# Neighbourhood attention in tiles of 16 grid rows by 8 grid columns, with every token layout following those tiles

## The chip, the cores and the metric

The kernel runs on one core of one Trainium2 chip. The time is the device time of one execution in microseconds (us): three runs of the kernel before gave a median of 2781.56 us, from 2779.58 to 2782.93 us. The profiled execution took 2779.84 us; its span, from the first to the last instruction, is 2778.1 us, so 1.7 us lie around the span.

## The reference, cut to what matters

One encoder layer is applied to 1024 prompt tokens (a grid of 16 rows by 64 columns) and, apart from them, to 256 sample tokens (4 rows by 64 columns). All arithmetic is float32, and the kernel gets it from pairs of rounded numbers (a high and a low part).

```
h = rms_norm(x);  qA,kA,vA,qB,kB,vB = split(h @ w_in)             # 1024 -> 6 x 512
# A: neighbourhood attention, 8 heads of 64; per token 8 grid rows x 16 grid columns of keys
row_start = clip(r - 4, 0, rows - 8);  col_start = clip(c - 8, 0, 64 - 16)
s = q.k / 8 + rpb[h, key_row - r + 7, key_col - c + 15];  outside the window: -inf
yA = rms_norm(softmax(s) @ v)
# B: differential attention, 4 heads, all tokens of the sequence are keys
s = q.k / 8 + t5_table[bucket(k_pos - q_pos)]                     # depends on the distance alone
yB = rms_norm((softmax(s1) - lam * softmax(s2)) @ v)
x = x + concat(yA, yB) @ w_out
x = x + expert_choice(rms_norm(x))      # 16 experts, each takes its 2n/16 best tokens
y = rms_norm(x)
```

`top_k` in the router keeps the lower token number where two affinities are equal, so the kernel has to count chosen tokens in the order of their numbers.

## The kernel before, in words

Tokens are handled in `TT` = 10 tiles of 128: prompt tiles 0 to 7 (128 consecutive tokens, that is two grid rows) and sample tiles 8 and 9. The program goes through these stages: load and normalise the ten tiles of `x` and turn them (`x_tile`, `x_tile_turn`); the values of half the heads (`v_tile`); the projection of keys and queries for the first job (`project(0, c, ...)`); then 80 attention steps, the output projection with router, the choice of tokens, and 16 experts, which take the last 1.9 ms.

A step `s` is one tile `t = s % 10` of one job `j = s // 10`. Jobs 0 to 3 are neighbourhood attention (`s < NAS`, two heads a job), jobs 4 to 7 differential attention. The order on TensorE in a neighbourhood step is written out: `scores(s)`, `values(s - 2)`, half of `project_part` (a share of the next job's key and query projection), `turn_exps(s - 1, ...)` (transposes of the exponentials in groups of at most 4 blocks, each into one of two buffers `PT`), the other half of `project_part`, and `out_turn(s - 2)`. VectorE adds the bias table and takes the maximum (`bias_max`), ScalarE takes the exponentials (`exps`), copies the turned blocks (`turned_copy`) and rounds weights (`w_round`). ScalarE and VectorE also go through the steps in a fixed order: in steps with `t` in (6, 7) of job `j`, ScalarE rounds the two halves of the unit of weights `(j + 2, 1)`, after the exponentials and copies of that step, and everything behind it on ScalarE waits for it.

How many keys a step has is set by `na_window(t)`. Two grid rows of queries see at most nine grid rows of keys, 576, for tiles 2 to 5; tiles 0, 1, 6 and 7 see 512; sample tiles see 256. Keys are taken by blocks of 128, the last block of a 576-key step being half full.

The bias of neighbourhood attention is laid out in memory as `G_d` (`bias_rows`), written once from GpSimd (L1920), and read back per job by `na_table(j)` on the SyncE queue as four loads into `TE` (L529). GpSimd adds the column mask and copies the nine rows of inner tiles to `TI` (`bias_tables`). The table of differential attention is a row of 2048 numbers a head, `F_d` (`t5_rows`), written from GpSimd as four rows of 2048 numbers (L1925), spread to `Fs_d` (`t5_shifted`), from which `df_table(h)` reads 128 rows of 1920 numbers in one load (L532).

The SyncE queue issues its transfers one after another in the order of the code. `unit(...)` loads one 512 KB piece of `w_in` into the single buffer `w_st` (L495), after the piece before it has been split (`w_split`); `w_round` waits for the load by the count of `w_in`.

After the output projection the chosen tokens are counted on TensorE (L883, `count`): one matmul with a triangular matrix inside tiles, and matmuls with a matrix of ones for the tiles before.

Of the kernel before, what the change touches and what calls it, by code (L numbers as in the profile page):

```python
# [8 lines left out]
F32 = mybir.dt.float32  # L9
# [6 lines left out]
P = 128  # L16
# [6 lines left out]
GW = 64  # L23
# [22 lines left out]

def na_window(t):

    if t >= TPR:
        return TPR, NSA, 7 - 2 * (t - TPR), False  # L50
    if t < 2:
        return 0, 512, 7 - 2 * t, False
    if t < 6:
        return t - 2, 576, 3, True
    return 4, 512, 3 - 2 * (t - 6), False


def na_blocks(t):
    return -(-na_window(t)[1] // P)
# [121 lines left out]
def build(nc, x_prompt, x_sample, mix_norm_w, w_in, na_rpb, na_norm_w, t5_table, lambda_q1,  # L181
# [10 lines left out]
    Fs_d = nc.dram_tensor("t5_shifted", (DF_H, P, 2 * NPR + P), F32).ap()  # L192
# [7 lines left out]
    def x_rows(t):  # L200
        return xp[t * P:(t + 1) * P, :] if t < TPR else xs[(t - TPR) * P:(t - TPR + 1) * P, :]
# [43 lines left out]
    TE = [at(f"TE{b}", [P, 2, 16, GW], F32, (150 + 8 * b) * K) for b in range(2)]  # L245
    TI = at("TI", [P, 2, 9 * GW], F32, 166 * K)
    BT = [at("BT0", [P, 1920], F32, 166 * K), at("BT1", [P, 1920], F32, 150 * K)]
    E0 = 173 * K + 512
    En = at("En", [P, 4, 640], F32, E0)
# [13 lines left out]
    t5_p = at("t5_p", [DF_H, 2 * NPR], F32, 80 * K)  # L263
    msk_w = at("msk_w", [P, 8, GW], F32, E0 + 29 * K)
# [4 lines left out]
    mask = after("mask", [P, GW], F32)  # L269
    ssx = after("ssx", [P, 2 * TT], F32)  # L270
# [40 lines left out]
    one = at("one", [P, P], BF16, 77 * K + 896)  # L311
    g_rest = at("g_rest", [P, TT, NE], F32, 79 * K)
# [68 lines left out]
    G_out, F_out, Fs_out = sem("G_out"), sem("F_out"), sem("Fs_out")  # L381
# [20 lines left out]
    te_in, bt_in = [sem("te_in0"), sem("te_in1")], [sem("bt_in0"), sem("bt_in1")]  # L402
    table_ready, te_clear = sem("table_ready"), sem("te_clear")
# [76 lines left out]
    with nc.Block() as block:  # L480
# [3 lines left out]
        def _(sp):  # L484
# [13 lines left out]
            def x_tile(t):  # L498
                if t >= 4:
                    sp.wait_ge(turned, 2 * (t - 3))  # L500
                sp.dma_start(xin[t % 4], x_rows(t)).then_inc(x_in[t % 4], 16)
# [36 lines left out]
            unit((1, 0), (2, 1), (2, 0))  # L538
# [6 lines left out]
            sp.wait_ge(scores_read, 2 * (3 * TT + 6))  # L545
            sp.wait_ge(Fs_out, 16)
# [3 lines left out]
            df_table(1)  # L550
            unit((5, 0), (6, 1), (6, 0))
            sp.wait_ge(scores_read, 2 * (NAS + TT))
            df_table(2)
            unit((7, 1), (7, 0))
            sp.wait_ge(scores_read, 2 * (NAS + 2 * TT))
            df_table(3)

# [7 lines left out]
            def mixed_rows(t):  # L565
# [3 lines left out]
                sp.dma_start(xt[:, t % 2, :], x_rows(t)).then_inc(y_in[t % 2], 16)  # L569
# [48 lines left out]
        def _(pe):  # L618
# [56 lines left out]
            def scores(s):  # L675
# [7 lines left out]
                if s < NAS:  # L683
                    kt0, nk, _, inner = na_window(t)
# [14 lines left out]
            def exp_blocks(s):  # L699
# [6 lines left out]
                return [En[:, 2 * (s % 2) + hf, b * P:min(nk, (b + 1) * P)] for hf in range(2) for b in range(na_blocks(t))]  # L706
# [13 lines left out]
            def values(s):  # L720
# [6 lines left out]
                if s < NAS:  # L727
                    kt0, nk, _, _ = na_window(t)
                    nb = na_blocks(t)
                    for b in range(nb):  # L730
                        n = min(P, nk - b * P)
                        for hf in range(2):
                            mm = pe.matmul(O[64 * hf:64 * hf + 64, 0:P],
                                           V[0:n, kt0 + b, cols.start + 64 * hf:cols.start + 64 * hf + 64],
                                           PTs[0:n, hf * nb + b, :], start=(b == 0), stop=(b == nb - 1))
# [33 lines left out]
            for s in range(NAS):  # L769
# [7 lines left out]
                if s >= 1:  # L777
                    turn_exps(s - 1, (2,))
# [107 lines left out]
            for t0, t1 in ((0, TPR), (TPR, TT)):  # L886
                for t in range(t0, t1):
                    if t + 1 < t1:
                        count(ranks[:, :, t + 1:t1, :], one,
                              chosen[:, :, t, :].unsqueeze(2).to_broadcast([P, 2, t1 - t - 1, NE]))  # L890
                    mm = count(ranks[:, 1, t0:t1, :], one,
                               chosen[:, 0, t, :].unsqueeze(1).to_broadcast([P, t1 - t0, NE]), last=t == TT - 1)
# [480 lines left out]
        def _(dve):  # L1373
# [49 lines left out]
            def window_mask():  # L1423
                dve.wait_ge(const_ready, 1)
                A, C = msk_w[:, 0, :], msk_w[:, 1, :]
# [80 lines left out]
            def na_bias(s):  # L1506

                j, t = s // TT, s % TT
                _, nk, row, inner = na_window(t)
# [8 lines left out]
                for hf in range(2):  # L1518
                    e = En[:, 2 * (s % 2) + hf, :]
                    if inner:  # L1520
                        bias_max(s, hf, S[:, hf, :].rearrange("p (b n) -> p b n", b=2)[:, :, 0:288],
                                 TI[:, hf, :].rearrange("p (b n) -> p b n", b=2),
                                 e[:, 0:576].rearrange("p (b n) -> p b n", b=2))
                    else:
# [657 lines left out]
```

## Time and profile before

| engine | busy, us | share of the span |
|---|---|---|
| TensorE (PE) | 2678.6 | 96% |
| TensorE weight loads (PEld) | 2521.4 | 91% |
| VectorE (DVE) | 1978.8 | 71% |
| ScalarE (ACT) | 1715.2 | 62% |
| GpSimd (POOL) | 1096.0 | 39% |

Profiled execution 2779.84 us, span 2778.1 us, mean granted TensorE clock 0.986 of full speed. The forty neighbourhood steps run from 112.4 us to about 348 us of the span; a job (ten steps) takes 59.2 us once it is steady. The differential steps begin at 409.8 us, the experts at about 862 us.

How to read it: "busy" is time in which an instruction was under way; a matmul's end is modelled and its length overlaps the next one, so what a group of matmuls costs is read from the start of the group to the start of the next. SyncE's own row does not count as busy; what it issues is seen as transfers.

### The profile page before, as it was taken

How to read it: one execution, taken by the hardware profiler on the slowest of the kernel's cores; microseconds unless marked ns; L12 is line 12 of the kernel's file. 1: busy time of each engine (PE TensorE's matmuls, PEld its weight loads, DVE VectorE, ACT ScalarE, POOL GpSimd, SP SyncE). 2: the span in 40 equal slices, each digit the busy share in tenths (PEclk: the TensorE clock that was granted, in tenths of full speed). 3: DMA queues.
4: the chain of work that ended last, by engine and by line, in shares of the span. 5: the costliest groups of instructions: out<-in, count | busy, mean ns of one | idle time of the engine just before them, and what ended most of it. 6: DMA issues, size and time to landing. Idle time of an engine off the chain costs nothing. (4 is left out here: it accounts for less than half of the span.)

```text
span 2778.1 us, 54432 instructions
## 1 busy us (share of the span) xinstructions
PE 2678.6 (96%) x22988; PEld 2521.4 (91%) x22988; DVE 1978.8 (71%) x2350; ACT 1715.2 (62%) x2559; POOL 1096.0 (39%) x738
## 2 busy tenths in 40 slices
PE   7999999998986999999999999999999999999996
PEld 7877898877876999999999999999999999999996
DVE  5233326666467878878788787887878788787787
ACT  3366615555124676767667676676767767676675
POOL 2132220224112453636446263452735436364352
PEclk9999999999987999999999999999999999999998
DMA  7231110113354889889888898879888888898887
GB/s 190 52 101 40 48 55 30 40 56 104 139 225 163 311 277 332 285 316 318 289 308 285 318 315 309 314 260 335 300 308 313 286 321 285 318 315 289 321 284 282
DMA packets 357644, 655.40 MB, mean 236 GB/s; under 512 B 25752, under 2 KB 85016, under 8 KB 356888
## 3 DMA queue, kind: packets, MB, share of 16 engines
q1 hardware_dynamic: 341291, 606.41, 61.2%
q0 software_dynamic: 16112, 45.53, 6.1%
q8 instruction: 183, 3.00, 0.4%
q14 instruction: 58, 0.47, 0.0%
HBM read 616.48 MB, written 39.62 MB: 236 GB/s over the span
## 5 line engine op out<-in xcount | busy, mean ns | idle before, releaser
L1776 DVE TENSOR_TENSOR wl<-stg,wh 128x2048 bf16<-128x2048 f32 (+1 forms) x544 | 1243.9, 2292 | 276.5 <-ACT wh L1298 271.9
L1298 ACT ACTIVATE wh<-stg 128x2048 fp32r<-128x2048 f32 (+1 forms) x544 | 1010.9, 1861 | 203.4 <-PE S L944 78.9
L2120 POOL TENSOR_TENSOR hx<-hh,hx 128x320 fp32r<-128x320 f32 x176 | 384.8, 2186 | 814.7 <-ACT hx L1350 814.4
L941 PE MATMUL S<-X,wh 128*128 128x320 f32 x3760 | 591.9, 312 | 1.3 <-DVE X L1785 1.3
L941 PEld LDWEIGHTS S<-X,wh 128*128 128x128 f32 x3760 | 556.3, 188 | 3.9 <-issue 2.1
L987 PE MATMUL S<-hx,wh 128*128 128x320 f32 x1892 | 312.4, 313 | 4.9 <-DVE yTs L1824 4.9
L941 PE MATMUL OG<-X,wh 128*128 128x320 f32 x1872 | 298.4, 312 | 0.0
L944 PE MATMUL S<-Xb,wl 128*128 128x160 bf16 x3760 | 290.1, 233 | 0.0
L987 PEld LDWEIGHTS S<-hx,wh 128*128 128x128 f32 x1892 | 280.8, 188 | 6.8 <-issue 6.7
L941 PEld LDWEIGHTS OG<-X,wh 128*128 128x128 f32 x1872 | 277.2, 188 | 1.3 <-issue 1.1
L944 PEld LDWEIGHTS S<-Xb,wl 128*128 128x128 bf16 x3760 | 258.9, 98 | 12.0
L2122 POOL CAST hb<-hx 128x320 bf16<-128x320 f32 x176 | 202.9, 1153 | 0.0
L1350 ACT ACTIVATE hx<-hh 128x320 fp32r<-128x320 f32 x176 | 83.1, 472 | 176.0 <-DVE hh L1813 176.0
L1968 POOL TENSOR_TENSOR ca<-lsum,half 128x20 f32<-128x20 f32 (+3 forms) x10 | 24.2, 2420 | 393.6 <-ACT o_all L1191 241.0
L987 PE MATMUL OG<-hx,wh 128*128 128x320 f32 x924 | 158.0, 313 | 1.9 <-DVE yTs L1824 1.9
L944 PE MATMUL S<-hb,wl 128*128 128x160 bf16 x1892 | 158.8, 233 | 0.0
L1159 ACT ACTIVATE E<-E,nmax 128x1024 f32<-128x1024 f32 (+1 forms) x80 | 81.8, 1023 | 110.0 <-DVE nmax L1503 110.0
L944 PE MATMUL OG<-Xb,wl 128*128 128x160 bf16 x1872 | 149.2, 233 | 0.0
L630 PE MATMUL OG<-hT_h,wkq 128*128 128x512 f32 (+1 forms) x384 | 149.1, 388 | 0.1
L987 PEld LDWEIGHTS OG<-hx,wh 128*128 128x128 f32 x924 | 138.6, 188 | 2.6 <-issue 2.6
L944 PEld LDWEIGHTS S<-hb,wl 128*128 128x128 bf16 x1892 | 132.1, 98 | 8.1
L632 PE MATMUL OG<-hT_h,wkq 128*128 128x512 f32 (+1 forms) x384 | 136.9, 356 | 0.0
(283 smaller groups left out, 4262.4 us busy)
## 6 DMA issues: line engine op xcount, KB each, us to landing
stg<-in_w_gate_dram SPq DMA_DIRECT2D x80, 2048.0 KB
stg<-in_w_up_dram SPq DMA_DIRECT2D x80, 2048.0 KB
stg<-in_w_down_dram SPq DMA_DIRECT2D x64, 2048.0 KB
stg<-in_w_down_dram SPq DMA_DIRECT2D x32, 1536.0 KB
stg<-in_w_gate_dram SPq DMA_DIRECT2D x16, 1024.0 KB
stg<-in_w_up_dram SPq DMA_DIRECT2D x16, 1024.0 KB
w_st<-in_w_in_dram SPq DMA_DIRECT2D x20, 512.0 KB, 3.8
yt<-mixed SPq DMA_DIRECT2D x10, 512.0 KB, 4.5
```

What stands on the lines that cost most here:

```text
L630: pe.matmul(out, lhs_h, rhs_h, start=first, stop=False)
L632: return pe.matmul(out, lhs_l, rhs_h, start=False, stop=last)
L941: pe.matmul(out, w, x, start=first, stop=False, skip_group_check=True)
L944: return pe.matmul(out[:, 0:CT], w, x, start=False, stop=last, skip_group_check=True)
L987: mm = pe.matmul(down_bank(e, d), whk[:, f, c * P:(c + 1) * P], hx[:, f0 + f, :], start=(f0 + f == 0), stop=(last and f0 + f == FT - 1), s ...
L1159: act.activation(e, e, ACT.Exp, scale=-1.0, bias=nmax[:, col:col + 1], accum_out=lsum[:, j % 2, t, hf:hf + 1]).then_inc(exp_done, 1)
L1298: act.activation(piece_conv(wh, g), piece_stage(g), ACT.Copy).then_inc(rounded, 1)
L1350: act.activation(hx[:, j - 1:j + 1, 0:CT], hh[:, :, :], ACT.Copy).then_inc(hidden_hi, 1)
L1776: dve.tensor_tensor(piece_conv(wl, g), piece_stage(g), piece_conv(wh, g).bitcast(F32), ALU.subtract).then_inc(split, 1)
L1968: own(pool.tensor_tensor(a, ls, minus_one, ALU.pow))
L2120: pool.tensor_tensor(hx[:, f, CT:2 * CT], hh[:, :, :], hx[:, f, 0:CT].bitcast(F32), ALU.subtract).then_inc(hidden_ready, 1)
L2122: pool.tensor_copy(hb[:, f, :], hx[:, f, 0:CT].bitcast(F32)).then_inc(hidden_b, 1)
```

## The change

Prompt tiles 0 to 7 become blocks of 16 grid rows by 8 grid columns (an octet of columns each). A tile's queries then see the keys of its own octet and its neighbours: 384 keys, or 256 for the first and last tile. The tokens of a tile come by a rearranged load of `x`, and results of the output projection are stored back by the rearranged pattern. The bias tables become: `TB`, five variants of 128 by 128 a head, put together from `TR`, which is loaded by 16 small loads a head; `TS` for the sample tiles; for differential attention `W_d` (`t5_octets`), written from `F_d` by 32 transfers of 31 x 15 runs of 8 numbers, from which `df_table` now loads its table in 16 pieces; and `BS` for the sample tiles. The counting of chosen tokens goes by grid rows inside and across tiles.

```diff
 def na_window(t):
     if t >= TPR:
-        return TPR, NSA, 7 - 2 * (t - TPR), False
-    if t < 2:
-        return 0, 512, 7 - 2 * t, False
-    if t < 6:
-        return t - 2, 576, 3, True
-    return 4, 512, 3 - 2 * (t - 6), False
+        return TPR, NSA
+    first, last = max(t - 1, 0), min(t + 1, TPR - 1)
+    return first, (last - first + 1) * P
+def row_start(r):
+    return min(max(r - NA_KH // 2, 0), GR - NA_KH)      # GR = 16, OC = 8
...
+    W_d = nc.dram_tensor("t5_octets", (DF_H, OC, 2 * TPR - 1, 2 * GR - 1, OC), F32).ap()
+    Fs_d = nc.dram_tensor("t5_shifted", (DF_H, P, NSA + 3 * P), F32).ap()
-    Fs_d = nc.dram_tensor("t5_shifted", (DF_H, P, 2 * NPR + P), F32).ap()
+    def octet(prompt, sample, t):
+        if t < TPR:
+            return prompt.rearrange("(r g c) d -> g r c d", r=GR, c=OC)[t]
+        return sample[(t - TPR) * P:(t - TPR + 1) * P, :]
...
             def na_table(j):
                 for hh_ in range(2):
+                    q = (2 * j + hh_) * NDR
                     for up in range(2):
-                        q = (2 * j + hh_) * NDR
-                        src = G_d[:, q:q + NDR, GW - 1:2 * GW - 1]
-                        sp.dma_start(TE[j % 2][GW * up:GW * up + GW, hh_, up:up + NDR, :], src).then_inc(te_in[j % 2], 16)
+                        sp.dma_start(TS[j % 2][GW * up:GW * up + GW, hh_, :, :],
+                                     G_d[:, q + 5 - up:q + 11 - up, GW - 1:2 * GW - 1]).then_inc(te_in[j % 2], 16)
+                    for r in range(GR):
+                        r0 = row_start(r)
+                        d0 = q + r0 - r + NA_KH - 1
+                        sp.dma_start(TR[j % 2][OC * r:OC * r + OC, hh_, r0:r0 + NA_KH, :],
+                                     G_d[0:OC, d0:d0 + NA_KH, GW - 1 - OC:GW - 1 + 2 * OC]).then_inc(te_in[j % 2], 16)
+            def t5_octets(h):
+                for c in range(OC):
+                    src = bass.AP(F_d.tensor, F_d.offset + h * 2 * NPR + OC - 1 - c,
+                                  [[GW, 2 * GR - 1], [OC, 2 * TPR - 1], [1, OC]])
+                    sp.dma_start(W_d[h, c].rearrange("g r k -> r g k"), src).then_inc(W_out, 16)
             def df_table(h):
-                sp.dma_start(BT[h % 2][:, :], Fs_d[h, :, P - 1:P - 1 + 1920]).then_inc(bt_in[h % 2], 16)
+                for r in range(GR):
+                    sp.dma_start(BT[h % 2][OC * r:OC * r + OC, :].rearrange("c (g q) -> c g q", q=P),
+                                 W_d[h, :, :, GR - 1 - r:2 * GR - 1 - r, :].rearrange("c g r k -> c g (r k)")
+                                 ).then_inc(bt_in[h % 2], 16)
...
             na_table(0)
             na_table(1)
-            unit((1, 0), (2, 1), (2, 0))
+            unit((1, 0))
+            sp.wait_ge(F_out, 16)
+            for h in range(DF_H):
+                t5_octets(h)
+            unit((2, 1), (2, 0))
...
-                    k0, chunks = kt0 * P, [(0, 0, 288), (512, 288, 288)] if inner else [(0, 0, nk)]
+                    k0, chunks = kt0 * P, [(0, 0, nk)]
...
                 project_part(s, 1)
-                if s >= 1:
-                    turn_exps(s - 1, (2,))
...
-            for t0, t1 in ((0, TPR), (TPR, TT)):
-                for t in range(t0, t1):
-                    if t + 1 < t1:
-                        count(ranks[:, :, t + 1:t1, :], one, ...)
-                    mm = count(ranks[:, 1, t0:t1, :], one, ..., last=t == TT - 1)
+            for t in range(TPR):
+                if t + 1 < TPR:
+                    n = TPR - t - 1
+                    count(ranks[:, 0, t + 1:TPR, :], one, chosen[:, 0, t, :].unsqueeze(1).to_broadcast([P, n, NE]))
+                    count(ranks[:, 1, t + 1:TPR, :], row_le, chosen[:, 1, t, :].unsqueeze(1).to_broadcast([P, n, NE]))
+                if t:
+                    count(ranks[:, 1, 0:t, :], row_lt, chosen[:, 1, t, :].unsqueeze(1).to_broadcast([P, t, NE]))
+                count(ranks[:, 1, 0:TPR, :], one, chosen[:, 0, t, :].unsqueeze(1).to_broadcast([P, TPR, NE]))
+            # the two sample tiles are counted as before: three matmuls
...
             def bias_tables(j):
-                pool.wait_ge(te_in[j % 2], 64 * (j // 2 + 1))
+                pool.wait_ge(te_in[j % 2], 16 * 2 * (2 + GR) * (j // 2 + 1))
...
+                own(pool.tensor_tensor(te, te, mask[:, :].unsqueeze(1).to_broadcast([P, 12, GW]), ALU.add))
+                for b, u, side in ((0, 0, None), (1, 0, 0), (2, 1, None), (3, 2, 1), (4, 2, None)):
+                    # one copy or one masked addition of 128 x 256 into TB
```

SyncE, from the weight loads ahead of the first bias tables on, before (a row names the line, the destination and source tensors, the shape of the destination and the count; `w_st` is the weight buffer, `TE` the bias table of a job):

```order
L495 DMA w_st<-in_w_in_dram 128x8x128 [waits w_split] x2
L529 DMA TE_71<-bias_rows 64x15x64 [waits te_clear,G_out]
L529 DMA TE_71<-bias_rows 64x15x64 x3
L529 DMA TE_72<-bias_rows 64x15x64 x4
L495 DMA w_st<-in_w_in_dram 128x8x128 [waits w_split] x3
```

The same place with the change, where `TS` and `TR` are parts of a job's tables and `t_octets` is `W_d`:

```order
L518 DMA w_st<-in_w_in_dram 128x8x128 [waits w_split] x2
L551 DMA TS_73<-bias_rows 64x6x64 [waits te_clear,G_out]
L551 DMA TS_73<-bias_rows 64x6x64
L556 DMA TR_75<-bias_rows 8x8x24 x16
L551 DMA TS_73<-bias_rows 64x6x64 x2
L556 DMA TR_75<-bias_rows 8x8x24 x16
L551 DMA TS_74<-bias_rows 64x6x64 x2
L556 DMA TR_76<-bias_rows 8x8x24 x16
L551 DMA TS_74<-bias_rows 64x6x64 x2
L518 DMA w_st<-in_w_in_dram 128x8x128 [waits w_split]
L564 DMA t_octets<-t_rows 31x15x8 x31
L518 DMA w_st<-in_w_in_dram 128x8x128 [waits w_split] x2
```

Eight loads ahead of unit (1, 0) have become 72, and between unit (1, 0) and unit (2, 1) stand 32 transfers from memory to memory that were not there (the first of them, and the last group of `TR`, are left out of the fence).

TensorE, scores and values of step 5 of job 0, before (`K_h` and `K_l` are the key parts, `PTs` the turned exponentials):

```order
L695 MATMUL S<-K_h,Qh 128x288 [waits fill_split,scores_read]
L695 MATMUL S<-K_h,Qh 128x288
L695 MATMUL S<-K_l,Qh 128x288 x2
L695 MATMUL S<-K_h,Ql 128x288 x2
L695 MATMUL S<-K_h,Qh 128x288 x2
L695 MATMUL S<-K_l,Qh 128x288 x2
L695 MATMUL S<-K_h,Ql 128x288 x2
L733 MATMUL OG<-PTs,V 64x128 [waits out_read,turned_copied]
L733 MATMUL OG<-PTs,V 64x128 x9
```

The same step with the change:

```order
L745 MATMUL S<-K_h,Qh 128x384 [waits fill_split,scores_read]
L745 MATMUL S<-K_h,Qh 128x384
L745 MATMUL S<-K_l,Qh 128x384 x2
L745 MATMUL S<-K_h,Ql 128x384 x2
L781 MATMUL OG<-PTs,V 64x128 [waits out_read,turned_copied]
L781 MATMUL OG<-PTs,V 64x128 x5
```

Twelve score matmuls of 288 columns are now six of 384, and ten value matmuls are six; the waits at the head of each group are the same.

## Rows read from the trace of the kernel before

**Rows 1.** Busy time by stretch: PE, PEld, DVE, ACT, POOL, clock, DMA share, GB/s.

```profile
170.00:229.00 59.00, 59.00 (x479) 47.45 (x478) 18.41 (x50) 38.39 (x132) 20.65 (x14) 1.00 0.20 46
...
840.00:2778.00 1938.00, 1892.11 (x17402) 1854.36 (x17402) 1575.67 (x1470) 1332.85 (x1518) 905.27 (x523) 0.99 0.85 300
```

**Rows 2.** Timeline of PE, first scores and job 1: start, length, what.

```profile
112.40 0.50 PE L695 MATMUL S<-K_h,Qh 64*128 64x512 f32 x2
...
169.94 0.50 PE L695 MATMUL S<-K_h,Qh 64*128 64x512 f32 x2
...
170.84 0.66 PE L733 MATMUL OG<-PTs,V 128*64 128x128 f32 x8
171.43 0.50 PE L630 MATMUL OG<-hT_h,wkq 128*128 128x512 f32 x1
...
180.38 0.40 PE L695 MATMUL S<-K_h,Qh 64*128 64x288 f32 x2
...
181.37 1.09 PE L733 MATMUL OG<-PTs,V 128*64 128x128 f32 x16
182.39 0.50 PE L630 MATMUL OG<-hT_h,wkq 128*128 128x512 f32 x1
...
200.19 1.46 PE L733 MATMUL OG<-PTs,V 128*64 128x128 f32 x20
201.58 0.50 PE L630 MATMUL OG<-hT_h,wkq 128*128 128x512 f32 x1
...
205.32 0.38 PE L625 MATMUL PT<-identf,En 128*128 128x128 f32 x2
205.54 0.27 PE L625 MATMUL PT<-identf,oTs 128*128 128x128 f32 x1
...
218.44 0.39 PE L695 MATMUL S<-K_h,Qh 64*128 64x256 f32 x2
...
218.99 1.09 PE L733 MATMUL OG<-PTs,V 128*64 128x128 f32 x16
...
229.18 0.50 PE L695 MATMUL S<-K_h,Qh 64*128 64x512 f32 x2
```

**Rows 3.** Timeline of the SyncE queue, issues from the constants to the first tables.

```profile
35.15 0.43 SPq L518 DMA_DIRECT2D lam_v<-in_lambda_q_dram  x1
...
78.46 9.18 SPq L529 DMA_DIRECT2D TE<-bias_rows  x8
106.75 54.89 SPq L495 DMA_DIRECT2D w_st<-in_w_in_dram  x3
```

**Rows 4.** The line of the table loads: ns of one issue, min/median/max.

```profile
L529 SPq DMA_DIRECT2D TE<-bias_rows x16: 585/774/1576, 78.5 to 228.1; - x16
```

**Rows 5.** The line that rounds weights on ScalarE, in job 0.

```profile
L1099 ACT ACTIVATE wkq<-w_st x4: 622/638/659, 121.7 to 159.9; 128x512 fp32r<-128x512 f32 x4
```

**Rows 6.** Timeline of ScalarE, end of step 6 of job 0.

```profile
154.28 0.66 ACT L1099 ACTIVATE wkq<-w_st 128x512 fp32r<-128x512 f32 x1
```

**Rows 7.** Timeline of GpSimd: the mask added to the first bias table.

```profile
86.98 4.60 POOL L1939 TENSOR_TENSOR TE<-TE,mask 128x2048 f32<-128x2048 f32 x1 [27.10 <-DMA TE<-bias_rows]
```

**Rows 8.** Transfers by size (columns as Rows 1): w_st; TE; w_st with BT.

```profile
186.00:195.00 9.00, 9.00 (x87) 7.07 (x85) 3.58 (x9) 5.81 (x22) 8.55 (x5) 1.00 0.21 60
165.50:174.50 9.00, 9.00 (x74) 7.58 (x72) 2.99 (x10) 5.51 (x22) 0.00 (x0) 1.00 0.63 109
338.00:346.00 8.00, 8.00 (x71) 6.69 (x66) 2.75 (x10) 4.99 (x19) 0.00 (x0) 1.00 0.53 190
```

**Rows 9.** The page's issues: KB each, median us from issue to landing.

```profile
w_st<-in_w_in_dram SPq DMA_DIRECT2D x20, 512.0 KB, 3.8
...
bias_rows<-rpb_p POOLq DMA_DIRECT2D x1, 3840.0 KB, 29.1
...
t_rows<-t_p POOLq DMA_DIRECT2D x1, 32.0 KB, 14.0
```

**Rows 10.** Timeline of PE, the counting of chosen tokens.

```profile
844.49 1.89 PE L883 MATMUL S<-chosen,one 128*128 128x224 bf16 x18
```

More of the change, by code:

```diff
@@ L705, in exp_blocks @@
                 nk = na_window(t)[1]
-                return [En[:, 2 * (s % 2) + hf, b * P:min(nk, (b + 1) * P)] for hf in range(2) for b in range(na_blocks(t))]
+                return [En[:, 2 * (s % 2) + hf, b * P:(b + 1) * P] for hf in range(2) for b in range(nk // P)]
             def turn_exps(s, fills):
@@ L885, in _ @@
             count(S[:, 1, 0:2 * TT * NE], tri, chosen[:, :, :, :].rearrange("p m t e -> p (m t e)"), first=True)
-            for t0, t1 in ((0, TPR), (TPR, TT)):
-                for t in range(t0, t1):
-                    if t + 1 < t1:
[L889 to L892, printed above, removed]
+            for t in range(TPR):
[6 more added lines that the diff above has]
+                count(ranks[:, 1, 0:TPR, :], one, chosen[:, 0, t, :].unsqueeze(1).to_broadcast([P, TPR, NE]))
+            for t in range(TPR, TT):
+                if t + 1 < TT:
+                    count(ranks[:, :, t + 1:TT, :], one,
+                          chosen[:, :, t, :].unsqueeze(2).to_broadcast([P, 2, TT - t - 1, NE]))
+                mm = count(ranks[:, 1, TPR:TT, :], one,
+                           chosen[:, 0, t, :].unsqueeze(1).to_broadcast([P, TT - TPR, NE]), last=t == TT - 1)
             mm.then_inc(pos_ps, 1)
@@ L1508, in na_bias @@
                 j, t = s // TT, s % TT
-                _, nk, row, inner = na_window(t)
+                nk = na_window(t)[1]
                 if t == 0:
@@ L1901, in _ @@
             own.wait()
+            own(pool.iota(msk_c[:, :], [[0, GR], [1, OC]], base=0, channel_multiplier=0,
+                          allow_small_or_imprecise_dtypes=True))
+            own.wait()
             pool.sem_inc(const_ready, 1)
@@ L1934, in bias_tables @@
             def bias_tables(j):
-                pool.wait_ge(te_in[j % 2], 64 * (j // 2 + 1))
+                pool.wait_ge(te_in[j % 2], 16 * 2 * (2 + GR) * (j // 2 + 1))
                 pool.wait_ge(mask_ready, 1)
-                te = TE[j % 2][:, :, :, :].rearrange("p h r c -> p (h r) c")
-                own(pool.tensor_tensor(te, te, mask[:, :].unsqueeze(1).to_broadcast([P, 32, GW]), ALU.add))
-                own.wait()
-                if j:
-                    pool.wait_ge(scores_read, 2 * ((j - 1) * TT + 6))
-                stand()
-                for h in range(2):
-                    own(pool.tensor_copy(TI[:, h, :], TE[j % 2][:, h, 3:12, :].rearrange("p r c -> p (r c)")))
-                own.wait()
-                stand()
-                own(pool.memset(TI[0:GW, :, 8 * GW:9 * GW], MASKED))
-                own(pool.memset(TI[GW:P, :, 0:GW], MASKED))
+                stand()
+                te = TS[j % 2][:, :, :, :].rearrange("p h r c -> p (h r) c")
+                tr = TR[j % 2][:, :, :, :].rearrange("p h r u -> p (h r) u")
+                own(pool.tensor_tensor(te, te, mask[:, :].unsqueeze(1).to_broadcast([P, 12, GW]), ALU.add))
+                for b, u, side in ((0, 0, None), (1, 0, 0), (2, 1, None), (3, 2, 1), (4, 2, None)):
+                    out = TB[j % 2][:, b, :, :].rearrange("p h (r c) -> p (h r) c", c=OC)
+                    cols = tr[:, :, OC * u:OC * u + OC]
+                    if side is None:
+                        own(pool.tensor_copy(out, cols))
+                    else:
+                        own(pool.tensor_tensor(out, cols,
+                                               mask_lr[:, side, :].unsqueeze(1).to_broadcast([P, 2 * GR, OC]), ALU.add))
                 own.wait()
@@ L2013, in list_constants @@
                 own(pool.memset(one[:, :], 1.0))
+                own(pool.memset(row_le[:, :], 1.0))
+                own(pool.memset(row_lt[:, :], 1.0))
                 own(pool.memset(posm[:, :, NE:NE + 2], 0.0))
@@ L2032, in list_constants @@
                 own(pool.memset(NG[:, :, NE:NE + 2, 2:PARTS], 0.0))
+                own.wait()
+                for rows, base in ((row_le, OC), (row_lt, 0)):
+                    own(pool.affine_select(out=rows[:, :], in_=rows[:, :], compare_op=ALU.is_gt, fill=0.0, base=base,
+                                           pattern=[[OC, GR], [0, OC]], channel_multiplier=-1))
                 own.wait()
```

105 lines of the change are left out of this document (71 added, 34 removed).

## The prediction

> **What bounds the kernel now.** Read the busy times by stretch first. In the second job of neighbourhood attention TensorE is busy for 59.00 of 59.00 us, while VectorE has 18.41, ScalarE 38.39 and GpSimd 20.65; the experts, 1938 us of the span, have TensorE busy for 1892 us [rows 1]. So in the stretch that the change touches, the other engines hide behind TensorE, and a matmul that goes is time that goes, as long as no wait takes its place. The experts are the same code on the same shapes; I take their time as unchanged. The second view is TensorE's timeline, read from the start of one group to the start of the next [rows 2]. The third is SyncE: it issues in order, so what stands ahead of a weight load delays it [rows 3]. The fourth is where those weight loads are waited for on ScalarE [rows 5, 6].
>
> **What TensorE saves.** Per neighbourhood step, from [rows 2]:
> - Scores to the next group: 0.90 us with 512 keys (169.94 to 170.84), 0.99 with 576 (180.38 to 181.37), 0.55 with 256 (218.44 to 218.99). For 384 I take the middle of 256 and 512, 0.725.
> - Values: 0.59 us for two blocks (170.84 to 171.43; the trace counts two passes a matmul, so x8 is two blocks for two heads), 1.02 for four (181.37 to 182.39), 1.39 for five with the half one (200.19 to 201.58). Three blocks: 0.805.
> - Transposes: 0.22 for two (205.32 to 205.54), 0.11 each; four, two or four of them go.
>
> A job has two tiles that go from 512 keys to 256, two from 512 to 384, four from 576 to 384, and two sample tiles that stay. Scores: 2 x 0.35 + 2 x 0.175 + 4 x 0.265 = 2.11. Values: 2 x 0.43 + 2 x 0.215 + 4 x 0.585 = 3.63. Transposes (eight to four, eight to six, ten to six): 2 x 0.44 + 2 x 0.22 + 4 x 0.44 = 3.08. That is 8.8 us a job and 35.3 us for four jobs. Could another engine take over? ScalarE's 38.4 us a job is below the 59.2 - 8.8 = 50.4 that a job would last (59.2 from 169.94 to 229.18 [rows 2]), and its exponentials and copies shrink too; VectorE and GpSimd are further off [rows 1]. No loss there.
>
> **What is added.** Counting: the 18 matmuls with ones took 1.89 us, 0.105 each [rows 10]. There are now 3 + 6 x 4 + 2 = 29 for the prompt and 3 for the sample, 14 more, and VectorE waits for the last: +1.5 us. The first load of x is now a pattern of 16 x 8 rows; an issue may cost the 0.77 us of a table load instead of 0.43 [rows 3, 4]: +0.3 us at the start. GpSimd's extra constants stand ahead of the third output tile, and rearranged stores keep rows of 4 KB: nothing, covered by output-projection matmuls, at most 1 or 2 us.
>
> So without a new wait: 2779.8 - 35.3 + 1.5 + 0.3 = 2746.3 us. The profiled execution lies 1.7 us under the median of the runs, within their spread, so I make no correction.
>
> **SyncE's queue.** The eight table loads were issued from 78.46 on [rows 3]. Now 8 TS loads at 0.77 us (6.2 us) [rows 4] and 64 TR loads at 0.47 us from issue to issue (0.43 and a gap, the nearest small load) [rows 3], 30.1 us: the last at 114.8. The first job's half is out at 96.6. With 5 us to land and GpSimd's work (4.60 us for 2048 columns makes 1.7 for the 768 of TS, and about 0.5 for each of five pieces of 256 columns) [rows 7], the table stands at about 106, ahead of the first scores at 112.4 [rows 2]. Unit (1, 0) goes out at 115 instead of 106.75 and lands 3.8 us later [rows 3, 9], at 119, just ahead of its first use at 121.7 [rows 5]. Both hidden, with 2 to 6 us to spare.
>
> Then come the 32 transfers of `t5_octets`, 31 x 15 = 465 runs of 32 bytes each: 14,880 packets. Unit (2, 1) stands behind all of them, and ScalarE wants it at the end of step 6. That was at 154.28 [rows 6]; by then TensorE has saved about 6 us, so at 148. All that ScalarE does behind this rounding waits with it: the exponentials of step 7 and the copy that frees `out_turn`. TensorE stops within one step.
>
> What does a packet cost? By DMA share times 16 engines times the stretch [rows 8]: 0.21 x 144 = 30.2 us for the 1024 packets of 512 bytes of `w_st`, 29.5 ns each; 0.63 x 144 = 90.7 us for the 3840 packets of 256 bytes of `TE`, 23.6 ns; 0.53 x 128 = 67.8 us, less 30.2 for a `w_st`, for the 128 rows of 7680 bytes of `BT`, 294 ns. The line through 256 and 512 bytes gives 18.4 ns at 32 bytes; the line through 512 and 7680 gives 11.8. Upper bound: the 7680 runs of 512 bytes that `bias_rows` wrote to memory took 29.1 us with all overhead [rows 9], 480 an engine, 61 ns. I take 18.4, from the sizes nearest to 32 bytes.
>
> How many engines share them? No row shows a transfer whose outer dimension is 31. Dealt evenly over 16 engines the packets last 14,880 x 18.4 / 16 = 17 us, and the 32 issues (25 us at 0.77) are what one sees. All on one engine they last 274 us. The row nearest to the question is `t_rows`: four rows, 32 KB, 14.0 us to landing, where 512 KB in 128 rows take 3.8 us [rows 9]. Its queue also held the tail of `bias_rows`, so it proves little, but it does say that a transfer with a small or odd outer dimension can't be taken to spread as one of 128 rows does. 31 splits into equal parts only by 1 and 31, while the quick transfers have 64 or 128 rows, which 16 divides. I take one engine.
>
> The Trainium skill, "DMA: Bandwidth & Descriptors", section "Why a DMA increments its semaphore by 16 and not by 1", says that a transfer uses the largest number up to 16 that divides the outer dimensions of both sides. By that rule 31 gives one engine, always the lowest, and this term is the 274 us; if the rule did not hold here it would be the 17 us. No row shows either.
>
> The single engine's ring also holds its part of every later SyncE load, so unit (2, 1) can't land before it is drained: 115 + 274 + 4 = 393 us. Wanted at 148: a stall of 245 us, once. After it, `W_d` is complete, the later units and tables are a job ahead of their use, and differential attention finds its tables. The `BT` tables in 16 pieces of 120 runs of 512 bytes: 1920 x 29.5 ns, even on eight engines 7 us, and they have a job's time. Sum: 2746.3 + 245 = 2991 us.
>
> With 11.8 ns the packets last 176 us, the stall is 147 and the time 2893; with 61 ns they last 908, and the time is 3625. The same page's specification table asks for at least 512 bytes a transfer and says that below this the engine reads, modifies and writes. By that rule the 32-byte writes would cost more than the loads I extrapolate from; no row here shows a small store to memory by itself.
>
> **The rivals.**
> - The packets are spread over 16 engines (or nearly so). 25 us of issue from 115 on, unit (2, 1) lands at 144, four us ahead of 148: 2746 us, faster by 1.2%. For it: every transfer whose landing the page gives is quick for its size but `t_rows`. Against: 31.
> - The packets are spread, but the many issues cost more than I take, 0.77 us each as for table loads. The 72 last 55 us, the first table is ready at about 115 instead of 112.4 (+3), unit (1, 0) lands at 138 instead of 121 (+17, the larger one counts for both): about 2763, faster by 0.6%.
> - The saving isn't had: a short step is bound by the chain from scores over VectorE and ScalarE to the transposes. It speaks against it that TensorE never waited in the rows of job 1. Then 2780, no change, if the octets don't matter either.
> - On the other side of these stands the forecast itself, one mechanism: unit (2, 1) behind `t5_octets`, decisive from the point at which the drain lasts longer than 148 - 119 = 29 us, or 1.9 ns a packet on one ring, and slower overall from 66 us, 4.5 ns a packet.
>
> **How the numbers follow.** Chances: one engine, slower, 0.79 (its own range 2880 to 3300, from 11 to 39 ns a packet); spread and quick, 0.13; spread with late issues, 0.05; no saving, 0.03. The predicted time is that of the first, 2991 us. The range goes down to 2742 to take in the spread cases and up to 3300; what is left out is the single engine above 39 ns. Faster or slower is meant beyond 0.2%, 5.6 us, which is about what the measurement tells from no change: faster 0.18, same 0.03, slower 0.79.
>
> **What would show it.** Right: PE idle in one block near 145 us with ScalarE's `w_st` rounding waiting for a DMA; SyncE's issue of `t_octets` drawn out; DMA share near one sixteenth (0.06) through that stretch; neighbourhood jobs 2 to 4 at 50 to 51 us each. Wrong: `t_octets` landing within some 30 us of its issue; jobs that still last over 55 us; a new wait in the output projection or at the first scores. A stall of the right place with another length means that the price of a packet was off, nothing else.

## The result and the profile after

The changed kernel takes 2909.55 us (median of 4 runs, 2905.96 to 2910.76), the kernel before 2780.90 us in the 4 runs beside them (2779.58 to 2782.93). The ratio is 1.046, 95% interval 1.0442 to 1.0478: slower, as forecast, by 129 us where 211 were forecast. 2909.55 lies in the range of the one-engine case (2880 to 3300), near its lower end.

SyncE's queue after, at the place of [rows 3] (start, length, line and what; times in us):

```profile
81.17 1.30 SPq L551 DMA_DIRECT2D TS<-bias_rows  x2
82.52 5.74 SPq L556 DMA_DIRECT2D TR<-bias_rows  x16
...
104.34 5.73 SPq L556 DMA_DIRECT2D TR<-bias_rows  x16
110.12 0.40 SPq L518 DMA_DIRECT2D w_st<-in_w_in_dram  x1
110.56 175.60 SPq L564 DMA_DIRECT2D t_octets<-t_rows  x32
286.21 15.54 SPq L518 DMA_DIRECT2D w_st<-in_w_in_dram  x2
...
526.59 11.08 SPq L568 DMA_DIRECT2D BT<-t_octets  x16
537.71 0.98 SPq L573 DMA_DIRECT2D BS<-t_shifted  x2
538.74 51.75 SPq L518 DMA_DIRECT2D w_st<-in_w_in_dram  x3
```

The 32 octet copies hold SyncE for 175.60 us: 5.49 us each, 11.8 ns for each of the 14,880 packets. Unit (2, 1) goes out at 286.21. The last two copies had not landed by then: the last landings that the trace records for their semaphore `W_out` stand at 289.2 and 294.4 us. ScalarE could start on unit (2, 1) at 295.33, 9.1 us after its issue, where 3.8 is usual [rows 9]. What the queue's standstill does stands in the waits from 100 to 450 us (engine, tile and line that waited, what ended the wait; us in total, times, longest):

```profile
ACT wkq L1152 <- DMA w_st<-in_w_in_dram: 144.5, 1, 144.5
PE PT L675 <- ACT PTs L1223: 144.1, 1, 144.1
```

One wait of ScalarE for the weights, and one of TensorE of the same length. ScalarE's row answers to [rows 6]; TensorE's timeline has the end of the stall, and then the starts of two jobs, to be read against the 59.24 us of a job in [rows 2]:

```profile
295.33 0.63 ACT L1152 ACTIVATE wkq<-w_st 128x512 fp32r<-128x512 f32 x1 [144.49 <-DMA w_st<-in_w_in_dram]
```

```profile
298.94 0.45 PE L675 MATMUL PT<-identf,oTs 128*128 128x128 f32 x1 [144.13 <-ACT PTs L1223]
...
312.03 0.39 PE L745 MATMUL S<-K_h,Qh 64*128 64x256 f32 x2
...
363.01 0.39 PE L745 MATMUL S<-K_h,Qh 64*128 64x256 f32 x2
```

A job now lasts 50.98 us, 8.26 less than before. By stretch (columns as in [rows 1]):

```profile
150.00:296.00 146.00, 4.77 (x36) 3.51 (x32) 0.70 (x2) 1.47 (x7) 0.00 (x0) 0.53 0.13 6
296.00:303.00 7.00, 4.06 (x22) 3.12 (x23) 2.74 (x10) 4.46 (x18) 0.00 (x0) 0.50 0.06 14
303.00:309.00 6.00, 5.75 (x34) 4.41 (x34) 1.37 (x5) 2.10 (x8) 0.00 (x0) 0.79 0.25 74
```

In the stall the granted clock fell to the lower level, 0.5 or 1.2 GHz, and it was still there when TensorE had work again at 298.94. A mean of 0.79 from 303 to 309 puts its rise at about 305.5. These 6.6 us at half the clock cost some 3 us.

The whole difference of the two spans, 130.9 us, divides so (each part is the difference of a distance between two starts):

| stretch | before | after | difference |
|---|---|---|---|
| to the first scores | 112.40 | 115.11 | +2.7 |
| first scores to first differential scores | 297.43 | 412.06 | +114.6 |
| from there to the first output tile | 271.67 | 279.40 | +7.7 |
| output tiles, first to last | 135.98 | 140.45 | +4.5 |
| last output tile to the end | 1960.62 | 1961.98 | +1.4 |

The second line is 144.1 us of stall and some 3 us of low clock, less 33 us that the steps save. The third shows in the waits from 520 to 560 us: behind the 16 `BT` loads of 526.59 to 537.7 above, unit (5, 0) comes late, and TensorE waits 6.3 us in turn.

```profile
ACT wkq L1152 <- DMA w_st<-in_w_in_dram: 7.9, 1, 7.9
...
PE S L745 <- DVE nmax L1564: 6.3, 1, 6.3
```

The fourth is the load of `x` for the residual, by its line, after:

```profile
L619 SPq DMA_DIRECT2D xt<-in_x_prompt_dram x8: 547/548/624, 765.5 to 888.2; - x8
L619 SPq DMA_DIRECT2D xt<-in_x_sample_dram x2: 332/332/333, 904.2 to 919.5; - x2
```

An issue of 16 groups of 8 rows takes 548 ns, one of 128 rows in a run 332 (before it was 327 or 328 for both). `yt` is issued behind it, and TensorE waits for the pair of them (`y_in` counts both) 7.1 us on 5 tiles, where it had been 1.5 us on 3.

### The profile page after: what moved, and what is told of

Same layout as the page of the kernel before. It is cut to its first block and busy times, and to the rows that moved or that the text cites. A ratio compares the mean times of both kernels' runs of the same rounds, so it can differ in the third digit from the quotient of the medians.

```text
span 2909.0 us, 53806 instructions
## 1 busy us (share of the span) xinstructions
PE 2650.7 (91%) x22570; PEld 2496.3 (86%) x22570; DVE 1971.1 (68%) x2355; ACT 1691.5 (58%) x2535; POOL 1089.4 (37%) x750
## 5 line engine op out<-in xcount | busy, mean ns | idle before, releaser
L1458 DVE TENSOR_TENSOR wkq<-w_st,wkq 128x512 fp32r<-128x512 f32 x36 | 29.8, 839 | 182.5 <-ACT wkq L1152 182.5
L680 PE MATMUL OG<-hT_h,wkq 128*128 128x512 f32 (+1 forms) x384 | 149.4, 389 | 2.1 <-DVE Ql L1546 1.5
L675 PE MATMUL PT<-identf,oTs 128*128 128x128 f32 x40 | 11.2, 280 | 145.1 <-ACT PTs L1223 144.1
## 6 DMA issues: line engine op xcount, KB each, us to landing
stg<-in_w_down_dram SPq DMA_DIRECT2D x32, 1536.0 KB, 11.1
```

What stands on the lines that cost most here:

```text
L680: pe.matmul(out, lhs_h, rhs_h, start=first, stop=False)
L1458: dve.tensor_tensor(lo[:, k, :], w_st[:, k, :], hi[:, k, :].bitcast(F32), ALU.subtract).then_inc(w_split, 1)
```

## The experiments

**The outer dimension of the copies.** The same packets to the same places, with 15 outside instead of 31.

```diff
-                                  [[GW, 2 * GR - 1], [OC, 2 * TPR - 1], [1, OC]])
-                    sp.dma_start(W_d[h, c].rearrange("g r k -> r g k"), src).then_inc(W_out, 16)
+                                  [[OC, 2 * TPR - 1], [GW, 2 * GR - 1], [1, OC]])
+                    sp.dma_start(W_d[h, c], src).then_inc(W_out, 16)
```

> The changed kernel with one edit: the 32 copies of the octet tables are described with the 15 groups as their outer dimension and the 31 row distances inside, the same 465 packets of 32 bytes each, to the same places. Theory one (each copy goes wholly to one DMA engine because 31 divides by nothing up to 16 but 1): now 15 engines share a copy, the 175.6 us that SyncE stood in these issues becomes about 12 us of transfer beside some 13 us of issues, unit (2,1) lands before 140 and ScalarE no longer waits 144.1 us for it; 2909.5 less 144.1 and less about 3 us of half clock behind the stall is 2762, with 2756 to 2770 as the range. Theory two (a copy from device memory to device memory in 32-byte packets costs 11.8 ns a packet in the queue itself, however many engines share it): the issues still take about 5.5 us each, the wait stays 144 us and the time 2905 to 2913.

Measured: 2759.61 us (2757.62 to 2764.82, 4 runs); ratio to before 0.9921, interval 0.9905 to 0.9938. SyncE's queue:

```profile
109.79 33.16 SPq L564 DMA_DIRECT2D t_octets<-t_rows  x32
142.99 13.47 SPq L518 DMA_DIRECT2D w_st<-in_w_in_dram  x2
```

The 144 us are gone, and with them 150 us of time, so the number of packets was not what cost. The issues take 33 us, not the 13 that I expected; unit (2, 1) at 142.99 is in time for ScalarE, which rounds it at 149.90 without a wait. The steps from the first scores to the first differential scores last 264.73 us against 297.43: without the stall the change saves 32.7 us there.

**The same copies cut by rows.** Here the order of the packets stays and only the count of rows in a copy changes. 31 is cut into 16 and 15, then into 17 and 14, 20 and 11, 25 and 6. The count that the queue later waits for on `W_out` is doubled with the copies (not shown).

```diff
-                    sp.dma_start(W_d[h, c].rearrange("g r k -> r g k"), src).then_inc(W_out, 16)
+                    dst = W_d[h, c].rearrange("g r k -> r g k")
+                    sp.dma_start(dst[:GR], src[:GR]).then_inc(W_out, 16)      # GR = 16; then 17, 20, 25
+                    sp.dma_start(dst[GR:], src[GR:]).then_inc(W_out, 16)
```

> The changed kernel, in which each octet copy of 31 rows is issued as two, of 16 rows and of 15 rows, 64 issues instead of 32; source, destination, order of the packets and their number stay. Theory one (the count 31 alone puts a copy on one engine): 16 and 15 engines share them; 64 issues of 0.36 to 0.5 us are 23 to 32 us from 110.6, unit (2,1) is issued by 134 to 143 and lands by 140 to 150 where ScalarE wants it at 151 (295.3 less the 144.5 of waiting), so the wait is 0 to 3 us and the time 2762 to 2768. Theory two (the order in which the packets read and write memory, row distance first, makes them slow): 64 issues of 2.7 us, the wait stays about 144 us, 2905 to 2915.

> As the copies cut into 16 and 15 rows, but cut into 17 and 14: 17 is prime. Theory one (the largest divisor up to 16 of the row count is the number of engines): the 17 rows, 255 packets, go to one engine, at 11.8 ns 3.0 us, and the pair takes 3.0 to 3.8 us, 32 of them 97 to 122 us from 110. Unit (2,1) then lands at 211 to 236, ScalarE wants it at 150.5, the wait is 60 to 86 us where 16 and 15 rows left 16.5, and the time 2779.8 plus 44 to 69: 2823 to 2849. A rival in which 31 is slow for its size or its packets and not for its divisors: 17 rows cost about what 16 do, 2776 to 2790.

> As above with 20 and 11 rows. Theory one (divisors): 10 engines and 11 engines, 30 and 15 packets each, a pair at 1.5 to 2.0 us, 48 to 64 us in all, a wait of 16 to 33 us, 2779 to 2797. The rival that more than 16 rows that 16 does not divide go to one engine: 300 packets at 11.8 ns are 3.5 us, a pair 3.6 to 4.3 us, a wait of 79 to 103 us, 2842 to 2866.

> As above with 25 and 6 rows. Theory one (divisors): 5 engines for the 25 rows, 75 packets each, at 11.8 ns 0.9 us, and 6 for the others; a pair at 1.5 to 2.2 us, 48 to 70 us, a wait of 16 to 39 us, 2779 to 2803. The rival that more than 16 rows go to one engine: 375 packets are 4.4 us, a wait of 106 to 133 us, 2869 to 2896.

Measured, one run each (the wait is ScalarE's for unit (2, 1)):

| rows | largest divisors up to 16 | time | wait | landings recorded |
|---|---|---|---|---|
| 31 (the change) | 1 | 2909.55 | 144.5 | 64 for 32 copies |
| 17 and 14 | 1 and 14 | 2835.59 | 73.0 | 544 for 64 |
| 25 and 6 | 5 and 6 | 2783.50 | 18.8 | 416 for 64 |
| 20 and 11 | 10 and 11 | 2782.55 | 19.9 | 736 for 64 |
| 16 and 15 | 16 and 15 | 2779.82 | 16.5 | 1024 for 64 |
| 15 outside | 15 | 2759.61 | none | 512 for 32 |

17 rows cost 52 to 53 us more than 25 or 20 rows do, so it is neither the size nor that 16 is passed. What sets 17 apart is that nothing up to 16 but 1 divides it. The queue shows it for 17 and 14 rows (L565 issues the 17, L566 the 14 behind them), and ScalarE's row its price:

```profile
126.27 0.60 SPq L565 DMA_DIRECT2D t_octets<-t_rows  x1
126.93 2.44 SPq L566 DMA_DIRECT2D t_octets<-t_rows  x1
```

```profile
222.63 0.63 ACT L1154 ACTIVATE wkq<-w_st 128x512 fp32r<-128x512 f32 x1 [72.95 <-DMA w_st<-in_w_in_dram]
```

It is the next issue that is held up, while the 255 packets on one engine drain: 0.60 and 2.44 and the gaps make 3.1 us, and over all 32 pairs 3.4, where 255 times 11.8 ns is 3.0. With 20 and 11 rows no issue is held up in the steady run, and a pair takes 1.57 us:

```profile
126.68 0.74 SPq L565 DMA_DIRECT2D t_octets<-t_rows  x1
127.46 0.75 SPq L566 DMA_DIRECT2D t_octets<-t_rows  x1
128.25 0.74 SPq L565 DMA_DIRECT2D t_octets<-t_rows  x1
```

My expectation of 0 to 3 us of wait for 16 and 15 rows was wrong: I priced an issue at 0.36 to 0.5 us, from the table loads, and these took 0.57 and 0.81 us in most pairs (and 0.04 from one to the next), some 47 us for 64. A few took up to 2.4 us, and all of them 53 us, from 109.96 to 162.82.

The landings that the trace records for the semaphore `W_out` fit one rule for all six: with k the largest divisor up to 16, a copy leaves k + 1 records where k is under 16, and 16 where it is 16. 32 x 2 = 64; 32 x (2 + 15) = 544; 32 x (6 + 7) = 416; 32 x (11 + 12) = 736; 32 x (16 + 16) = 1024; 32 x 16 = 512. All six counts come out. The Trainium skill, "DMA: Bandwidth & Descriptors", section "Why a DMA increments its semaphore by 16 and not by 1", says that each engine in use posts one and the issuing sequencer writes the remaining 16 - k in one step; by that rule the counts are these, and the trace agrees.

**Half of the copies.** The tables of heads 2 and 3 are read from those of heads 0 and 1, so that 16 copies do.

```diff
-            for h in range(DF_H):
+            for h in range(DF_H // 2):
                 t5_octets(h)
...                                    # df_table(h) reads W_d[h % 2]
```

> The changed kernel with 16 of the 32 octet copies: only those of the first two heads are made, and the tables of heads 2 and 3 are loaded from those of heads 0 and 1 (their bias is that of another head). Theory one (a queue of work on one engine that the weights behind it wait out, 5.49 us a copy): the wait shrinks by 16 times 5.49, 87.8 us, from 144.1 to about 56, and the time to 2909.5 less 87.8, 2822, range 2815 to 2828. A rival in which the wait is a fixed one for the last copy's completion, or is ended by something else, gives 2895 to 2910.

Measured: 2818.04 us. The queue and the wait:

```profile
110.35 87.67 SPq L564 DMA_DIRECT2D t_octets<-t_rows  x16
198.06 15.58 SPq L518 DMA_DIRECT2D w_st<-in_w_in_dram  x2
```

```profile
ACT wkq L1152 <- DMA w_st<-in_w_in_dram: 56.6, 1, 56.6
```

5.48 us a copy again, and the wait shrinks by 87.9 us with 87.9 us less in the queue. That leaves 3.6 us of the 91.5 gained. The stretch from the differential scores to the first output tile is 276.38 us here and not 279.40, and ScalarE's wait for unit (5, 0) in it 5.4 us and not 7.9, which holds 3.0 of them; why that wait was shorter isn't shown.

**The kernel before with the copies added.** No tile is changed; nothing reads the result.

```diff
-            unit((1, 0), (2, 1), (2, 0))
+            unit((1, 0))
+            sp.wait_ge(F_out, 16)
+            for h in range(DF_H):
+                for c in range(8):
+                    src = bass.AP(F_d.tensor, F_d.offset + h * 2 * NPR + 7 - c, [[GW, 31], [8, 15], [1, 8]])
+                    sp.dma_start(W_d[h, c].rearrange("g r k -> r g k"), src).then_inc(W_out, 16)
+            unit((2, 1), (2, 0))
```

> The kernel before the change with one addition: the 32 octet copies of the change, in its form with 31 rows outside, behind unit (1,0) on SyncE's queue; nothing reads what they write, and the queue waits for them ahead of the first dilated table. Theory one (the copies alone make the loss, whatever the tiles are): SyncE stands about 175 us from about 109, less the slack before ScalarE wants unit (2,1); the time is 2780.9 plus 135 to 147 and 3 of half clock, 2918 to 2931. A rival (the loss needs the new tables' 70 small loads ahead of the copies, or the changed order of tiles): under 2850.

Measured: 2926.22 us, 144.7 over the kernel before. A copy took 5.74 us here, not 5.49.

```profile
107.36 183.62 SPq L545 DMA_DIRECT2D t_octets<-t_rows  x32
```

```profile
ACT wkq L1108 <- DMA w_st<-in_w_in_dram: 145.6, 1, 145.6
```

The copies alone make the loss; neither the new tiles nor the 72 table loads are needed for it.

**The copies as they were, from GpSimd's queue,** behind its second table.

```diff
-            for h in range(DF_H):          # SyncE
-                t5_octets(h)
+            for h in range(DF_H):          # GpSimd, behind bias_tables(1)
+                for c in range(OC):
...                                    # src as before
+                    pool.dma_start(W_d[h, c].rearrange("g r k -> r g k"), src).then_inc(W_out, 16)
```

> The changed kernel with its 32 copies as they are, 31 rows outside and one DMA engine each, but issued on GpSimd's queue, behind its second table, at about 116 us, in place of SyncE's. Theory one in its pure form (only what stands behind them in the same queue waits): SyncE issues unit (2,1) at once, ScalarE has it by 125, and the time is 2762 to 2770. Theory one with a price on GpSimd (its issues are held up as SyncE's were, 32 of 5.5 us until about 292): the table of job 2, wanted at about 216, is ready only at about 310, a wait of some 90 us there instead of 144, and the time 2840 to 2865. A rival in which the copies load the chip whatever queue they are on, the wait of 144 us stays: 2905 to 2915.

Measured: 2968.95 us, the worst of all. ScalarE did not wait for unit (2, 1); the wait of 144 us is gone. But GpSimd was held longer than SyncE had been (its timeline, then VectorE's):

```profile
116.51 6.64 POOL L2058 DMA_DIRECT2D t_octets<-t_rows  x2 [0.71 <-POOL TB L2007]
136.78 6.46 POOL L2058 DMA_DIRECT2D t_octets<-t_rows  x2 [13.63 <-issue]
...
398.63 6.46 POOL L2058 DMA_DIRECT2D t_octets<-t_rows  x2 [12.07 <-issue]
```

```profile
425.64 0.42 DVE L1554 CUSTOM_DVE_ANT_1 En<-S,TB 128x256 f32<-128x256 f32 x1 [208.93 <-POOLq L2012]
```

Each copy took 9.0 us there (289 us for 32), 3.2 of them as GpSimd's own work; the table of job 2 was late by 209 us. The mechanism of the second case, a table held up on GpSimd, was right and its price of 5.5 us a copy too low. Why a pair of issues is followed by 12 us without any stays open. SyncE's queue was not left alone either: 16 `TR` loads for job 2 took 12.1 and 15.0 us of it (from 164.05 and 177.51) where such a group had taken 5.7 to 6.1 ahead of the copies, so the pure form of theory one was wrong on this point too.

**Rows of x in their own order.** On the kernel with 15 outside; the tokens of a tile are then others than its tables assume.

```diff
-                sp.dma_start(xt[:, t % 2, :], octet(xp, xs, t)).then_inc(y_in[t % 2], 16)
+                sp.dma_start(xt[:, t % 2, :], straight(t)).then_inc(y_in[t % 2], 16)
```

(and the same for `xin` at the start)

> The kernel with the octet copies of 15 groups outside, in which the ten loads of x at the start and the ten in the output projection read rows of x in their own order, one run of 128 rows, not 16 groups of 8 rows (so the tokens of a tile are others than its tables assume, and the output is not the reference's). If the rearranged load is what costs, the first scores come 2.7 us earlier and the output loop takes 4.5 us less, 2752 us, range 2749 to 2756. If something else of the change does, nothing moves: 2758 to 2762.

Measured: 2758.22 us, one run: by its time alone no difference to the 2757.62 to 2764.82 of the kernel it is built on. The stretches tell more. The output tiles take 135.88 us, from 141.06; before they took 135.98, so the 4.5 us of the table above come with the rearranged load. ScalarE's first square starts at 4.36 us where it had been 6.11, 5.84 and 5.78 us with the rearranged load, and 4.54 before; the first scores come at 113.50, against 113.92 to 115.27 in the ten kernels that have the rearranged load, and 112.40 before. So 0.4 to 1.8 us of the 2.7 at the start are this load, and about one is not.

**Unit (5, 0) ahead of the second differential table.** On the kernel with 15 outside.

```diff
-            unit(("v", 1), ("v", 2), (5, 1))
+            unit(("v", 1), ("v", 2), (5, 1), (5, 0))
             sp.wait_ge(v_ready, V_END)
             df_table(1)
...
-            unit((5, 0), (6, 1), (6, 0))
+            unit((6, 1), (6, 0))
```

> The kernel with the octet copies of 15 groups outside, and unit (5,0) issued ahead of the wait for the v columns and the second dilated table, nothing else. If the 7.7 us between the first dilated scores and the output projection are the weights waiting behind 16 issues of 0.7 us, the stretch falls back to the 271.7 us of before and the time to 2752, range 2748 to 2756. If it was the tables that were late, the stretch stays near 279 us and the time near 2760.

Measured: 2753.43 us, one run. The row of the wait is gone, and the stretch from the differential scores to the first output tile is 268.47 us (271.67 before, 283.18 in the kernel it is built on, where the wait was 9.9 us). The profiled execution of that kernel was the slowest of its four, 2764.82 us, so the gain is better read from the times, 2759.61 and 2753.43: 6.2 us. How much of the wait was the 16 issues and how much their transfers isn't separated (in the changed kernel the unit went out at 538.74 and ScalarE began with it at 547.42). The 16 us in which that wait had fallen, without and with the edit:

```profile
396.00:412.00 16.00, 7.71 (x41) 5.88 (x40) 7.59 (x13) 6.69 (x17) 0.00 (x0) 0.68 0.38 70
```

```profile
396.00:412.00 16.00, 16.00 (x117) 13.49 (x114) 10.65 (x21) 11.40 (x29) 0.00 (x0) 1.00 0.22 50
```

The wait took the clock with it, 0.68 against 1.00 over these 16 us. TensorE stood 8.3 us, until 404.99, and the granted clock was 0.50 from then to 408 and 0.74 from 408 to 410, so that some 2 us come on top of its standstill.

**Both, and yt ahead of xt.** The edit above, and in the output projection the `yt` load ahead of the rearranged one, which gets a semaphore of its own for VectorE. TensorE no longer waits for `xt` at all.

```diff
-                sp.dma_start(xt[:, t % 2, :], octet(xp, xs, t)).then_inc(y_in[t % 2], 16)
                 sp.dma_start(yt[t % 2][:, :], y_d[t * P:(t + 1) * P, :]).then_inc(y_in[t % 2], 16)
+                if t:                      # tile 0 keeps its load of xt ahead
+                    sp.dma_start(xt[:, t % 2, :], octet(xp, xs, t)).then_inc(xt_in[t % 2], 16)
...
-                pe.wait_ge(y_in[t % 2], 32 * (t // 2 + 1))
+                pe.wait_ge(y_in[t % 2], 16 * (t // 2 + 1))
```

> The kernel with the octet copies of 15 groups outside (2759.6 us), with unit (5,0) issued ahead of the second dilated table, and in the output projection with each yt load issued ahead of the rearranged xt load of its tile, xt having a semaphore of its own for VectorE. From the trace of the changed kernel: moving the unit removes the 7.9 us in which ScalarE waited for its weights behind 16 table loads, and the order of the two loads brings TensorE's input 0.5 to 1.5 us earlier on some five tiles that waited 7.1 us in all for it; 2759.6 less 7.7 less 2 to 4.5 is 2748 to 2750, range 2744 to 2754. Rivals: the wait moves to the table (DVE waits for the second dilated table instead), 2758 to 2762.

Measured: 2750.75 us (2749.32 to 2751.25, 4 runs), ratio to before 0.9893, interval 0.9876 to 0.9909. The output tiles take 135.88 us with the rearranged load still there, and no wait for `yt` is left. So it was the load's place ahead of `yt`, or that TensorE waited for both; the edit changes the two together. The stretch ahead of the output tiles is 272.99 us here and was 268.47 in the kernel with unit (5, 0) moved alone, so only the sum of the two stretches compares: 408.87 against 411.15, a gain of 2.3 us (407.65 before). This beats both kernels: 30 us under before, 159 under the change as it was.

## Why the prediction was right, and where its sizes were off

**Right: the step that decided.** Unit (2, 1) behind `t5_octets`, the copies on one engine, ScalarE waiting at the end of step 6, TensorE stopped within a step. Four results bear it out: the stall at that place, its proportion to the number of copies, its transfer into the kernel before, and its end when the outer dimension has a divisor. That 31 goes to one engine was argued from its divisors; the times for 17, 20 and 25 rows and the landings now bear that out. That unit (2, 1) can't land before the copies have drained shows in its 9.1 us to landing. TensorE's idle block began at 154.8 us, behind the 145 that I named.

**Mis-sized: a packet.** I took 18.4 ns, by the line through the nearest sizes of [rows 8], and got 274 us; it was 11.8 ns and 175.6 us. That is the lower of my two lines, the one through 512 and 7680 bytes; the nearest sizes were the worse guide here. That it agrees to the first decimal is luck: the line starts from shares of two digits, and 0.20 instead of 0.21 for `w_st` would lower it by about 2 ns. Nor did the 32-byte writes cost more than that line, as I had held possible. Why the price is what it is isn't settled: those rows are of loads into SBUF over all engines, this is a copy within memory on one, and no run set the two apart. The stall came to 144.5 us instead of 245. My sum for 11.8 ns gave 147, and three of its terms were off in ways that nearly cancel: the copies began at 110.56 and not 115, ScalarE wanted the unit at 150.8 and not 148, and it landed in 9.1 us and not 4. By itself the shorter stall made the forecast 100 us too high; it was 81 too high in all (2991 less 2909.6), since the smaller terms below go the other way.

**Nearly right: the saving.** 8.26 us a job for 8.82, 32.7 in the whole stretch for 35.3. The prices of the pieces held. TensorE now is idle for 0.38 us a job (busy 50.60 of 50.98 us, where it had been 59.00 of 59.00). Most of that is one wait in the last step of a job, where VectorE isn't yet done with the queries' low part; here it is in the first job:

```profile
308.44 0.36 PE L680 MATMUL OG<-hT_h,wkq 128*128 128x256 f32 x1 [0.25 <-DVE Ql L1546]
```

**Missed: the clock.** The stall costs some 3 us beyond its length, since TensorE restarts at the lower level, 1.2 GHz. I had no term for it.

**Missed: the rest of SyncE's queue.** I counted seven us of transfer for the `BT` pieces and a job's time for them. What counted was what stands behind them: 16 issues, 11.1 us, ahead of a weight load without slack, +7.7. In the same way I costed the rearranged load of `x` at 0.3 us, for its first issue; it was 2.7 at the start, of which 0.4 to 1.8 are shown to be this load, and 4.5 in the output projection, where I had named only stores. I said "nothing, at most 1 or 2 us" for that place, and named a new wait there as a sign that I was wrong; it came, 7.1 us of it, beside a mechanism that held.

**Too high: counting and issues.** The 14 more matmuls cost 0.4 us, not 1.5. A TR load costs 0.36 us from issue to issue, not 0.47; the last went out at about 110.1, not 114.8, and unit (1, 0) was in time. By my own terms the change turns slower from a drain of 62.5 us on (29 and the 33.5 saved), not 66; nothing else used that figure.

**Wrong: a sign that I named.** I expected a DMA share of 0.06, one engine of 16, through the stall. It was 0.13, two engines' worth. The packets' times in the records overlap. The queues from 160 to 280 us (packets, MB, share of 16 engines):

```profile
q1 hardware_dynamic: 10218, 0.33, 11.7%
```

11.7% of 16 engines over 120 us is 22 ns for each of the 10,218 packets, while one came every 11.7 ns. So if one engine carries them, as the landings say, about two packets are under way on it at a time, and the share of busy time does not count engines.

## What to carry to other kernels

Before a transfer goes into an in-order queue, look at its outer dimension: here 31 and 17, primes above 16, put it all on one engine, the issues behind it were held up, and a load behind them landed only when the copies had drained. Turning the two dimensions, or cutting the rows so that each part has a large divisor, costs a line. Then ask of every group of small issues what is queued behind it and how much slack that has; here a group of 16 loads of 0.7 us cost 6 to 8 us, and the cure was to let the weight load pass them.

## What the runs showed of the hardware

- 32-byte packets from memory to memory in copies of 31 rows, which by their landings went to one engine, came every 11.8 ns; over 15 engines a copy of 465 of them still took 1.04 us of SyncE (33.16 us for 32), 2.2 ns a packet. With the larger part of a copy on 5, 10 or 16 engines the kernel's time was within 4 us, so there it was no longer the number of engines that limited but, as far as the queue's rows show, the issues.
- The same copy from GpSimd's queue took 9.0 us and left 16 landings a copy (512 for 32), so that the records there do not tell how many engines carried it.
- A load of 128 rows of 4 KB costs SyncE 0.33 us in one run and 0.55 us in 16 groups of 8 rows, and landed in 3.6 against 4.9 us (medians, with the two sample tiles among them).
